# Order of the wide and narrow products in the gated networks, and the form of the last up projection

## The reference, cut to what matters

```
def swiglu(x, w_in, w_out):
    h = x @ w_in
    gate, up = h[..., :D_FF], h[..., D_FF:]
    return (jax.nn.silu(gate) * up) @ w_out
...
f = (jax.nn.silu(h2 @ w_ffn_gate[l]) * (h2 @ w_ffn_up[l])) @ w_ffn_down[l]
```

## Time and profile before

| | |
|---|---|
| median of 3 runs | 1513.32 us |
| the profiled execution, span | 1511.2 us |
| TensorE busy | 1493.9 us (99%), 8200 matmuls |
| VectorE, ScalarE, GpSimd busy | 920.0, 792.0, 189.9 us |
| mean granted TensorE clock | 0.998 of full speed |

### The profile page before, as it was taken

How to read it: one execution, slowest core, us unless ns; L and a number is a source line. 1 busy time by engine, 2 the same in 40 slices (tenths; PEclk the granted TensorE clock), 3 DMA queues, 4 the chain that set the end, 5 groups by cost and what they waited for, 6 DMA issues and landing times.

```text
span 1511.2 us, 21617 instructions
## 1 busy us (share of the span) xinstructions
PE 1493.9 (99%) x8200; PEld 1293.6 (86%) x8200; DVE 920.0 (61%) x1192; ACT 792.0 (52%) x956; POOL 189.9 (13%) x56
## 2 busy tenths in 40 slices
PE   8999999999999999999999999999999999999997
PEld 6888888888888888898888888888888998888886
DVE  7475465666666566523776668766666455756667
ACT  5446545444444444666554456654446654544456
POOL 0014211000040000362100001000005441100010
PEclk9999999999999999999999999999999999999999
DMA  8545446655546555551565556565555434655562
GB/s 313 182 140 177 160 156 196 212 191 194 193 160 203 194 186 177 174 186 65 187 206 187 194 195 226 175 218 185 185 191 162 123 121 162 205 199 184 187 211 81
DMA packets 187258, 273.71 MB, mean 181 GB/s; under 512 B 10144, under 2 KB 137280, under 8 KB 187200
## 3 DMA queue, kind: packets, MB, share of 16 engines
q1 hardware_dynamic: 183136, 261.72, 51.6%
q10 hardware_dynamic: 4064, 11.18, 2.4%
HBM read 271.78 MB, written 1.05 MB: 181 GB/s over the span
## 4 chain that ended last, share of the span: by engine, by line
PE 94%; DVE 3%; ACT 2%; DMA 1%; issue 0%; SPq 0%; ACTq 0%; DVEq 0%
PE bank L694 23%; PE bank L696 12%; PE bank L551 8%; PE bank L553 7%; PE bank L552 7%; PE acc L551 7%; PE acc L552 7%; PE acc L553 7%; PE bank L726 3%; PE acc L853 2%; PE acc L547 2%; PE bank L608 2%; PE bank L601 2%; PE bank L616 2%; DVE tanh L1869 1%; DVE x L1890 1%
## 5 line engine op out<-in xcount | busy, mean ns | idle before, releaser
L1785 DVE TENSOR_TENSOR w_lo<-w_raw,w_hi 128x2048 fp32r<-128x2048 f32 (+2 forms) x209 | 475.2, 2278 | 163.1 <-ACT w_hi L1344 121.4
L694 PE MATMUL bank<-xT,w_hi 128*128 128x512 f32 x1520 | 380.0, 392 | 0.2 <-DVE w_lo L1785 0.2
L499 POOL TENSOR_TENSOR w_lo<-w_raw,w_hi 128x2048 fp32r<-128x2048 f32 (+1 forms) x41 | 176.7, 4316 | 1278.6 <-ACT w_hi L1262 1278.6
L694 PEld LDWEIGHTS bank<-xT,w_hi 128*128 128x128 f32 x1520 | 276.3, 189 | 52.4 <-DVE w_lo L1785 0.9
L1344 ACT ACTIVATE w_hi<-w_raw 128x2048 fp32r<-128x2048 f32 x145 | 276.4, 1907 | 0.0
L696 PEld LDWEIGHTS bank<-xT,w_lo 128*128 128x128 f32 x1520 | 207.4, 190 | 14.8
L696 PE MATMUL bank<-xT,w_lo 128*128 128x256 f32 x1520 | 211.9, 282 | 0.0
L1262 ACT ACTIVATE w_hi<-w_raw 128x2048 fp32r<-128x2048 f32 (+3 forms) x106 | 190.9, 1817 | 21.2 <-DMA w_raw<-in_w_in 11.4
L551 PE MATMUL acc<-w_hi,hTh 128*128 128x512 f32 x400 | 156.2, 391 | 0.0
L552 PE MATMUL acc<-w_lo,hTh 128*128 128x512 f32 x400 | 156.2, 391 | 0.0
L553 PE MATMUL acc<-w_hi,hTl 128*128 128x512 f32 x400 | 155.6, 389 | 0.0
(11 more groups left out here) (220 smaller groups left out, 2092.9 us busy)
## 6 DMA issues: line engine op xcount, KB each, us to landing
w_raw<-in_ffn_w_in SPq DMA_DIRECT2D x176, 512.0 KB, 4.4
w_raw<-in_ffn_w_out SPq DMA_DIRECT2D x88, 512.0 KB, 4.1
w_raw<-in_w_in SPq DMA_DIRECT2D x52, 512.0 KB, 4.6
w_raw<-in_fox_w_in SPq DMA_DIRECT2D x24, 512.0 KB, 4.5
w_raw<-in_w_ffn_gate SPq DMA_DIRECT2D x22, 512.0 KB, 4.4
w_raw<-in_w_ffn_up SPq DMA_DIRECT2D x22, 512.0 KB, 4.2
w_raw<-in_w_ffn_down SPq DMA_DIRECT2D x22, 512.0 KB, 4.1
w_raw<-in_ple_w_gate SPq DMA_DIRECT2D x16, 512.0 KB, 4.5
```

Of the source, the lines that this page charges most:

```text
L499: pool.tensor_tensor(w_lo[s][:, 0:cols], w_raw[u % RING][:, 0:cols], w_hi[s][:, 0:cols].bitcast(F32), ALU.subtract).then_inc(w_lo_done[u % ...
L694: pe.matmul(out, wh[:, k, m], both, start=k == 0, stop=False)
L1785: nc.vector.tensor_tensor(w_lo[s][:, 0:cols], w_raw[u % RING][:, 0:cols], w_hi[s][:, 0:cols].bitcast(F32), ALU.subtract).then_inc(w_lo_don ...
```

## The change

Inside a unit the products no longer alternate by half. The gate unit runs its 16 wide products and then its 16 narrow ones; the up unit runs its 16 narrow products first and then its 16 wide ones. `last_up` is gone: the last up unit has the same form as the others, in banks 2 and 3, with ScalarE's copy and VectorE's add behind it. The counts that TensorE and VectorE wait for on `u_summed` follow.

```diff
-                def wide(u, split, b):
+                def wide(u, split, b, narrow_first):
...
+                    def wides():
+                        for m in range(2):
+                            for k in range(KD):
+                                both = xT[:, k].rearrange("p a n -> p (a n)")
+                                mm = pe.matmul(bank[b + m], wh[:, k, m], both, start=k == 0 and not narrow_first,
+                                               stop=k == KD - 1 and narrow_first, skip_group_check=narrow_first)
+                        return mm
...
+                    if narrow_first:
+                        narrows()
+                        mm = wides()
+                    else:
+                        wides()
+                        mm = narrows()
                     mm.then_inc(w_used, 1)
...
-                    wide(u0 + 5, i + ((u0 - 1) // RING + 1), 0)
+                    wide(u0 + 5, i + ((u0 - 1) // RING + 1), 0, False)
...
-                    if last:
-                        last_up(u0 + 6, i + (u0 // RING + 1))
-                    else:
-                        wide(u0 + 6, i + (u0 // RING + 1), 2)
+                    wide(u0 + 6, i + (u0 // RING + 1), 2, True)
...
                     gate_tanh(i)
+                    crosses(2, i * 3 + (u0 + 1), u_sum, u_copied)
                     if last:
...
-                    crosses(2, i * 3 + (u0 + 1), u_sum, u_copied)
...
-                    if last:
-                        dve.wait_ge(w_used, i * 3 + (u0 + 1))
-                        hidden_up(i, halves(bank[2]))
-                    else:
-                        add_crosses(i + ups0, 2, u_sum, u_copied, u_summed)
-                        dve.wait_ge(u_summed, i + ups0)
-                        hidden_up(i, halves(u_sum))
+                    add_crosses(i + sums0, 2, u_sum, u_copied, u_summed)
+                    dve.wait_ge(u_summed, i + sums0)
+                    hidden_up(i, halves(u_sum))
```

More of the change, by code:

```diff
@@ new lines, in narrows @@
+                    def narrows():
+                        for m in range(2):
+                            for k in range(KD):
+                                mm = pe.matmul(bank[b + m][:, S:], wl[:, k, m], xTh[:, k], start=k == 0 and narrow_first,
+                                               stop=k == KD - 1 and not narrow_first, skip_group_check=narrow_first)
+                        return mm
+                    if narrow_first:
[4 more added lines that the diff above has]
+                        mm = narrows()
@@ L802, in ffn, with step @@
                 sums0 = f * (FI - 1) - 1
-                ups0 = f * (FI - 2) - 1
-                def step(i, first=False, last=False):
+                def step(i, first=False):
                     if not first:
                         pe.wait_ge(g_summed, i + sums0)
-                    wide(u0 + 5, i + ((u0 - 1) // RING + 1), 0)
+                    wide(u0 + 5, i + ((u0 - 1) // RING + 1), 0, False)
                     if first:
@@ L813, in step @@
                     else:
-                        pe.wait_ge(u_summed, i + ups0)
-                    if last:
-                        last_up(u0 + 6, i + (u0 // RING + 1))
-                    else:
-                        wide(u0 + 6, i + (u0 // RING + 1), 2)
+                        pe.wait_ge(u_summed, i + sums0)
+                    wide(u0 + 6, i + (u0 // RING + 1), 2, True)
                     if first:
@@ L831, in ffn @@
                     step(i)
-                step(FI - 1, last=True)
+                step(FI - 1)
                 u = u0 + 3 * FI - 2
@@ L1928, in ffn @@
                 sums0 = f * (FI - 1)
-                ups0 = f * (FI - 2)
                 def add_crosses(done, b, dst, copied, summed):
```

## The result

The kernel with the change takes 1517.24 us (median of 9 runs, 1516.88 to 1517.71), the kernel before 1513.39 us beside it (9 runs, 1513.23 to 1513.73). The ratio is 1.0024 with an interval of 1.0016 to 1.0033: 3.85 us slower. The forecast was 1516.4: the result lies inside its range of 1514.3 to 1518.0, and 0.04 above the 1515.7 to 1517.2 that the forecast had called its own. The profiled executions differ by 3.8 us (1515.0 against 1511.2), so the two traces can be compared term by term.

The account below looks back on a forecast made before the run. The prediction took TensorE, busy 99% of 1511.2 us, to bound the kernel. Its terms -2.7 - 1.2 + 6.97 gave +3.1 us, carried to 1513.32 as 1516.4 us, range 1514.3 to 1518.0.

Parts of the forecast that it names:

- The loop steps: 45 of the 50 network steps, first steps included: each 0.06 us shorter through the new order, 2.7 us in all.
- The first steps: Each network's first step: counted among the 45 at 0.06 us, with no difference from where the transposes stand.
- The bound that the longer narrow run eats the gain: In the steps, 32 narrow products in a row would leave a gain of 0, making the total +5.8 us.
- the third rival: The order brings nothing in the loop, as wide products behind 32 narrow ones start slower: +5.8, 1519.1 us; chance 0.13.
- The last step's products: Gate, up and down products of each network's last step: 0.24 us less each, 1.2 us in all.
- The hand-over: Each last step: the copy and add make TensorE wait 0.97 us, 1.11 with restart, 1.32 in networks 2 and 4.
- The tails of networks 1 to 4: Network ends: late by ScalarE's 1.36 or 1.57 us, through the rounding GpSimd waits for; with network 0's 1.11, 6.97 us.
- ScalarE's lateness: At each network's end, `hT_round` starts 1.36 us later against the first down product, 1.57 in networks 2 and 4.
- The pair of the norm: Two VectorE operations of line 1869 behind networks 1, 2 and 3: again some 3.5 us long, held up by GpSimd.
- TensorE's own wait alone reaches the end: Rival on the tails: GpSimd operations have slack, so only TensorE's wait counts: +2.1, 1515.4 us; chance 0.15.
- the tails give the wait back: Rival: slack behind the networks makes the hand-over cost less than the 3.9 us saved; 1509.4 us if none remains; chance 0.12.
- the two halves of the change: Product savings in all steps, 3.9 us, against the lateness at the five network ends, 6.97 us.

Follow-up runs that it names:

- the cover of 24 products: The changed kernel, but all 24 down products of part 9 go before the wait for `hT_rest`, instead of 12: 1516.41 us, ratio 1.0019.
- the late ScalarE: The kernel before, with two extra unread ScalarE copies behind the last `hT_round` of each network: 1517.42 us, ratio 1.0025.
- the last step's form alone: The kernel before, with only the last up unit made an ordinary one with copy and add, old product order kept: 1520.12 us, ratio 1.0043.
- the order alone: The kernel before, with only the new order of wide and narrow products, keeping the old `last_up` and its hand-over: 1510.66 us, ratio 0.9981.
- the exchanged units: The changed kernel, but behind networks 2 and 4 GpSimd takes the unit rounded early and VectorE the one behind `hT_round`: 1527.99 us, ratio 1.0097.
- units exchanged in the order alone: New product order with old `last_up`, plus GpSimd and VectorE swapping units behind networks 2 and 4: 1516.57 us, ratio 1.0021.
- the coarser alternation: The kernel before, but gate and up each take 16 wide products, then 16 narrow ones, with the old `last_up`: 1511.72 us, ratio 0.9987.

## Why the prediction was right

Forecast 1516.4 us, measured 1517.24, inside the range; the mechanism held and two sizes were a little small.

**The loop steps.** Predicted 0.06 us each (16.55), measured 16.55 in all eight of each network, 2.4 us. The first steps were to give 0.06 as well, 0.3 in all. From a step's first wide product to its first down product they are 0.02, 0.05, 0.09 and 0.05 us shorter in networks 0 to 3 and 0.05 longer in network 4: 0.16 in all. Those of networks 1 to 4 lie inside the tails of the table above, so the steps' own sum below is without them. The bound that the longer narrow run eats the gain is refuted, and with it the third rival: a wide group behind 32 narrow ones takes 3.65 us for 16 in three kernels' traces.

**The last step's products.** Predicted 0.24 us each, measured 16.79 - 16.55 = 0.24. Gains of 3.55 in place of 3.9.

**The hand-over.** The time line counted from the last up product came out to 0.01 us, and to 0.00 for TensorE's restart. The five waits are there. Network 0's tail is 1.05 us longer, predicted 1.11; with the cover of 24 products it went to -0.05, so that wait is its whole cause.

**The tails of networks 1 to 4.** Predicted 1.36, 1.57, 1.36 and 1.57, measured 1.47, 1.53, 1.66 and 1.61: 6.27 for 5.86. GpSimd's rest begins later against the first down product by 602.47 - 596.75 - (601.46 - 597.09) = 1.35 us in network 1, by 1.56 in network 2 and by 1.36 in network 3, so ScalarE's lateness was right to 0.01. In networks 1 and 3 some 0.1 us arises behind the norm. In network 1 it arises where the late ScalarE's 0.36 did: GpSimd's later `w_lo` begins 1.69 us later against the first down product, and TensorE, whose products there are 0.12 us apart, pauses for 0.35 (636.59 to 636.94). In network 3 it arises at the start of network 4, and its cause is open. The pair of the norm, predicted some 3.5 us long, took 3.78, 3.81 and 8.79 us. Network 3 has another 0.2, and that is a step that I had passed over: two operations of GpSimd meet the norm there. VectorE and GpSimd before,

```profile
1139.80 4.15 DVE L1869 SCALAR_TENSOR_TENSOR tanh<-x,neg_mean,gb 128x512 f32<-128x512 f32 x2
...
1143.25 5.18 POOL L499 TENSOR_TENSOR w_lo<-w_raw,w_hi 128x2048 fp32r<-128x2048 f32 x1 [0.51 <-ACT w_hi L1262]
...
1144.06 5.58 DVE L1890 SCALAR_TENSOR_TENSOR x<-tanh,rstd,gb 128x512 f32<-128x512 f32 x2
```

and after:

```profile
1140.69 4.62 POOL L499 TENSOR_TENSOR w_lo<-w_raw,w_hi 128x2048 fp32r<-128x2048 f32 x1 [221.77 <-ACT w_hi L1263]
...
1142.11 8.79 DVE L1870 SCALAR_TENSOR_TENSOR tanh<-x,neg_mean,gb 128x512 f32<-128x512 f32 x2
...
1145.57 4.78 POOL L499 TENSOR_TENSOR w_lo<-w_raw,w_hi 128x2048 fp32r<-128x2048 f32 x1 [0.25 <-ACT w_hi L1263]
...
1151.01 1.41 DVE L1891 SCALAR_TENSOR_TENSOR x<-tanh,rstd,gb 128x512 f32<-128x512 f32 x2
```

Before, the first pair came through between the two GpSimd operations, and the second pair waited for the second. After, the gap between them shrank, and part of the first pair waited for both: 8.79 us. The order of the starts decides it. Before, the pair's second operation began at 1143.21, 0.04 us ahead of GpSimd's, and took 0.74 us; after, it began at 1145.78, 0.21 us behind GpSimd's, and took 5.12. GpSimd's second end is only 0.69 us later against the first down product (its own operation is shorter), but more of VectorE's work is left behind that end: the second pair ends 1152.42 - 1150.35 = 2.07 us behind it, before 1149.64 - 1148.43 = 1.21. In all it ends 1.55 us later, where 1.36 was predicted.

**The rivals.** That TensorE's own wait alone reaches the end is refuted by the cover of 24 and, from the other side, by the late ScalarE. That the tails give the wait back is refuted by the last step's form alone, 1.0043. The sum: 0.35 us of gain less, 0.35 us of tails more and 0.04 at the start, together the 0.7 us between +3.1 and +3.8. Both misses point the same way; none of them was made good by another.

The prediction named the two halves of the change (-3.9 with the last step's products, +6.97) but gave no time for a kernel with only one of them. That is what mattered most: the order alone is 1510.66 us.

## What to carry to other kernels

Find out of each part of a change by itself what it does on the path: here a reordering gained 3 us and a tidier common form for the last unit lost 6.5, and together they hid each other. A unit that ends a phase should keep its own, shorter hand-over, though it costs more products: the products that the old form has more cost 0.85 us in all (0.17 a network), and the copy and add that it saves 7.4. When an engine is late, follow every consumer of its queue and not only the wait that you see: four of the five tails were set by the operation that ScalarE does next, for GpSimd. And before moving a GpSimd operation, list every two-operand SBUF operation of VectorE that can meet it, the one that TensorE waits for first. Where a change leaves TensorE idle for long, read the granted clock behind the idle time too: behind the exchanged units it made about a third of that experiment's loss.

## What the runs showed of the hardware

- A VectorE operation of 0.69 us took 4.59 us beside a GpSimd operation of 4.51 us that had begun 0.47 us ahead of it (`hT_rest`, GpSimd's and VectorE's unit exchanged), and a pair of 1.41 us took 8.79 us where two GpSimd operations followed each other by 0.26 us. GpSimd loses too: 5.52 us where it starts under VectorE's rest, 4.61 where it does not. Between two GpSimd operations the one that started first went first: a VectorE operation that began 0.04 us ahead of GpSimd's second took 0.74 us, one that began 0.21 us behind it took 5.12.
- With a weight load for each, products of 512 columns go at 0.227 us and of 256 at 0.120 us, at a granted clock of 0.998 to 0.999. Each return from narrow to wide costs 0.02 to 0.03 us once, as the experiment on the coarser alternation shows.
- Behind idle times of 4.91 us (two, units exchanged in the change) TensorE's granted clock was 0.50, for 3.2 and about 5 us, and products of 512 columns went at 0.43 us. Behind two of 1.9 us (units exchanged in the order alone) it was once 1.00 and once 0.50; behind the change's five of 0.81 and 1.01 us it was 1.00.
